# A hybrid decoder step on one core: the routing of the next expert moved from chunks 10 to 12 of a trip to chunks 3 to 7

## The reference

```python
def moe_swiglu(x, g, w_router, w_eg, w_eu, w_ed):
    h = rms_norm(x, g)
    hf = h.reshape(-1, D_MODEL)
    logits = (hf @ w_router).astype(jnp.float32)
    top_v, top_i = lax.top_k(logits, TOP_K)
    gates = jax.nn.softmax(top_v, axis=-1)
    combine = jnp.einsum('tk,tke->te', gates, jax.nn.one_hot(top_i, N_EXPERTS, dtype=jnp.float32)).astype(h.dtype)
    y = jnp.zeros_like(hf)
    for e in range(N_EXPERTS):
        he = jax.nn.silu(hf @ w_eg[e]) * (hf @ w_eu[e])
        y = y + combine[:, e:e + 1] * (he @ w_ed[e])
    return x + y.reshape(x.shape)
```

## Time and profile before

| | |
|---|---|
| median of three runs | 1713.35 us (1709.89 to 1715.0) |
| profiled execution: time, span | 1716.68 us, 1714.6 us |
| TensorE busy | 1556.1 us (91%), 7880 matmuls |
| VectorE busy | 1274.8 us (74%) |
| ScalarE busy | 959.4 us (56%) |
| GpSimd busy | 147.8 us (9%) |
| HBM read | 422.55 MB |
| mean granted TensorE clock | 0.939 of full speed |

### The profile page before, as it was taken

The page is one execution under the profiler, slowest core; times in us unless marked ns, Lnnn a source line. Parts: engine busy times, 40 slices in busy tenths (PEclk is TensorE's granted clock), DMA queues, the critical chain, the costliest instruction groups (busy, mean ns, idle before and its releaser), DMA issues.

```text
span 1714.6 us, 22193 instructions
## 1 busy us (share of the span) xinstructions
PE 1556.1 (91%) x7880; PEld 1305.6 (76%) x7880; DVE 1274.8 (74%) x1277; ACT 959.4 (56%) x999; POOL 147.8 (9%) x135
## 2 busy tenths in 40 slices
PE   6776899999978889979989979979997997997998
PEld 5764899999956868858868868868876885886886
DVE  5998645446784468868868868868886885886886
ACT  5411543344553357656656656657665765765664
POOL 5561111012210100000000000000000000000000
PEclk8888999999987889989989989999998998998999
DMA  8821245444450269969969969987996996996993
GB/s 316 152 94 54 74 148 183 150 144 166 146 206 1 77 258 355 346 248 355 358 263 352 354 249 364 353 320 289 347 349 246 352 354 240 357 353 249 352 350 140
DMA packets 64321, 431.38 MB, mean 252 GB/s; under 512 B 7861, under 2 KB 10165, under 8 KB 13712
## 3 DMA queue, kind: packets, MB, share of 16 engines
q1 hardware_dynamic: 57312, 412.38, 64.0%
q0 software_dynamic: 3616, 12.28, 3.1%
q10 hardware_dynamic: 3344, 6.05, 1.0%
HBM read 422.55 MB, written 9.14 MB: 252 GB/s over the span
## 4 chain that ended last, share of the span: by engine, by line
PE 79%; DVE 11%; DMA 4%; ACT 3%; issue 2%; POOL 1%; ACTq 0%; DVEq 0%; POOLq 0%
PE bank L333 24%; PE bank L335 23%; PE bank L334 23%; DMA xt<-h_rows,slot_row 3%; DVE odd L1173 2%; DVE C L1173 2%; DVE w_lo L1118 2%; PE bank L718 1%; PE bank L355 1%; DVE w_lo L1394 1%; ACT w_hi L1013 1%; PE bank L589 1%; PE bank L669 1%; DVE C L1186 1%; PE bank L700 1%
## 5 line engine op out<-in xcount | busy, mean ns | idle before, releaser
L1394 DVE TENSOR_TENSOR w_lo<-land,w_hi 128x2048 fp32r<-128x2048 f32 x224 | 504.0, 2288 | 106.3 <-ACT w_hi L1013 105.3
L1013 ACT CAST w_hi<-land 128x2048 fp32r<-128x2048 f32 x224 | 417.3, 1910 | 3.5 <-issue 3.5
L333 PE MATMUL bank<-w_hi,xe_hi 128*128 128x512 f32 x896 | 366.3, 409 | 0.6 <-DVE xe_lo L1478 0.6
L334 PE MATMUL bank<-w_lo,xe_hi 128*128 128x512 f32 x896 | 355.5, 397 | 0.0
L335 PE MATMUL bank<-w_hi,xe_lo 128*128 128x512 f32 x896 | 355.5, 397 | 0.0
L1016 ACT CAST d_hi<-land 128x2048 fp32r<-128x2048 f32 x112 | 214.0, 1911 | 117.2 <-PE bank L335 117.2
L1489 DVE TENSOR_TENSOR d_lo<-land,d_hi 128x2048 fp32r<-128x2048 f32 x112 | 256.7, 2292 | 30.5 <-ACT d_hi L1016 25.4
L335 PEld LDWEIGHTS bank<-w_hi,xe_lo 128*128 128x128 f32 x896 | 169.1, 189 | 40.8
L333 PEld LDWEIGHTS bank<-w_hi,xe_hi 128*128 128x128 f32 x896 | 169.6, 189 | 34.2 <-issue 1.0
L334 PEld LDWEIGHTS bank<-w_lo,xe_hi 128*128 128x128 f32 x896 | 169.8, 190 | 33.0
L333 PE MATMUL bank<-d_hi,heT_hi 128*128 128x512 f32 x448 | 184.1, 411 | 4.8 <-DVE heT_lo L1511 4.8
(11 more groups left out here) (243 smaller groups left out, 2221.9 us busy)
## 6 DMA issues: line engine op xcount, KB each, us to landing
land<-in_w_expert SPq DMA_DIRECT2D x336, 1024.0 KB, 5.2
land<-in_w_dense SPq DMA_DIRECT2D x54, 1024.0 KB, 4.8
rel_rows<-rb POOLq DMA_DIRECT2D x1, 3072.0 KB, 38.0
bias<-rel_rows ACTq DMA_DIRECT2D x4, 512.0 KB, 5.4
X<-in_x SPq DMA_DIRECT2D x4, 288.0 KB, 6.0
out_y<-X SPq DMA_DIRECT2D x2, 576.0 KB, 2.8
Us<-in_state POOLq DMA_DIRECT2D x1, 1088.0 KB, 9.4
out_conv_s<-Us POOLq DMA_DIRECT2D x1, 1088.0 KB, 6.5
```

Of the source, the lines that this page charges most:

```text
L333: pe.matmul(out, w[0], x[0], start=start, stop=False)
L334: pe.matmul(out, w[0], x[1], start=False, stop=False)
L1013: act.copy(w_hi[n % RING][:], land[(DENSE + u) % LAND][:]).then_inc(hi_done, 1)
L1394: dve.tensor_tensor(w_lo[n % RING][:], land[slot][:], w_hi[n % RING][:].bitcast(F32), ALU.subtract).then_inc(split, 1)
```

## The change

The constant `GATES_AT` becomes `TURN_AT = 3` and `SCATTER_AT = 10`. Within a trip:

- the transposes of `pick` stand at the end of chunk 3 (before: 10) and go to bank 4 in place of 7; TensorE no longer waits there for the eighth sum;
- `place(trip+1)` stands in chunk 4 (before: 11);
- `slot_rows` stands at the end of chunk 6 (before: 11) and goes to bank 5; it no longer waits for the copy of `PT`;
- `slot_row_of` stands in chunk 7 (before: 12) and GpSimd's fetch follows it; it also copies the gate to a new tile `next_gate`, from which `slot_gate` is written at the end of the trip, in place of a read of bank 7;
- ScalarE's copy to `PT` stands in chunk 10 (before: 11) and waits for the eighth `back` to be done (semaphore `y_done`), since `back` reads the old `PT` up to then;
- TensorE waits for that copy before `gather` writes bank 4 in chunk 13.

```diff
-GATES_AT = KT_D + 2
+TURN_AT = 3
+SCATTER_AT = KT_D + 2
...
+               ("slot_gate", [SLOTS, 1], F32), ("next_gate", [SLOTS, 1], F32), ("slot_of", [P, 3, PASSES * NE + 1], F32),
...
             def turn_picks():
                 for j, (t0, nt) in enumerate(TT):
-                    last = pe.transpose(bank[7][:, t0:t0 + nt], pick[0:nt, j, :], ident[0:nt, 0:nt])
+                    last = pe.transpose(bank[4][:, t0:t0 + nt], pick[0:nt, j, :], ident[0:nt, 0:nt])
...
                         with pe.If(trip < n_trips - 1):
+                            pe.wait_ge(PT_ready, trip + 2)
                             gather(trip + 1, 0)
...
-                    if ch == GATES_AT:
-                        pe.wait_ge(y_added, trip * KT_D + KT_D)
+                    if ch == TURN_AT:
                         turn_picks()
-                    if ch == GATES_AT + 1:
+                    if ch == TURN_AT + 3:
                         with pe.If(trip < n_trips - 1):
                             pe.wait_ge(P_ready, trip + 2)
-                            pe.wait_ge(PT_ready, trip + 2)
-                            slot_rows(bank[7])
+                            slot_rows(bank[5])
...
-                    if ch == GATES_AT + 1:
+                    if ch == SCATTER_AT:
                         act.wait_ge(PT_done, trip + 1)
-                        act.copy(PT[:, :], bank[7][:, 0:T]).then_inc(PT_ready, 1)
+                        act.wait_ge(y_done, trip * KT_D + KT_D)
+                        act.copy(PT[:, :], bank[4][:, 0:T]).then_inc(PT_ready, 1)
...
                 dve.wait_ge(rows_placed, n)
+                dve.tensor_copy(next_gate[:], src[:, 1:2]).then_inc(gate_kept, 1)
                 dve.tensor_scalar(slot_row[:], src[:, 0:1], -1.0, float(T), ALU.mult, ALU.add).then_inc(rows_ready, 1)
...
-                    if ch == GATES_AT + 1:
+                    if ch == TURN_AT + 1:
                         with dve.If(trip < n_trips - 1):
                             dve.wait_ge(PT_done, trip + 1)
                             place(trip + 1)
...
-                    if ch == GATES_AT + 2:
+                    if ch == TURN_AT + 4:
                         with dve.If(trip < n_trips - 1):
-                            slot_row_of(trip + 2, bank[7])
+                            slot_row_of(trip + 2, bank[5])
...
                     dve.wait_ge(oe_ready, trip * 2 + 4)
-                    dve.tensor_copy(slot_gate[:], bank[7][:, 1:2]).then_inc(gates_ready, 1)
+                    dve.wait_ge(gate_kept, trip + 2)
+                    dve.tensor_copy(slot_gate[:], next_gate[:]).then_inc(gates_ready, 1)
```

More of the change, by code:

```diff
@@ L174, in build @@
                ("PT", [SLOTS, T], F32R), ("tok", [P, 3, 2], F32), ("slot_row", [SLOTS, 1], I32),
-               ("slot_gate", [SLOTS, 1], F32), ("slot_of", [P, 3, PASSES * NE + 1], F32),
+               ("slot_gate", [SLOTS, 1], F32), ("next_gate", [SLOTS, 1], F32), ("slot_of", [P, 3, PASSES * NE + 1], F32),
                ("gate_of", [P, 3, PASSES * NE + 1], F32), ("lg", [P, 6, 3, NE], F32), ("rt", [P, 3], F32),
                ("cmp", [P, 2, 3, NE, NE], F32), ("top", [P, 16], F32), ("trips", [1, 2], I32)]
-        (d_hi0, d_hi1, d_lo0, d_lo1, oe_hi, oe_lo, pick, PT, tok, slot_row, slot_gate, slot_of, gate_of, lg, rt,
+        (d_hi0, d_hi1, d_lo0, d_lo1, oe_hi, oe_lo, pick, PT, tok, slot_row, slot_gate, next_gate, slot_of, gate_of, lg, rt,
          cmp_, top, trips, xe_hi, xe_lo, xt, silu_g, he, heT_hi, heT_lo) = phase(
@@ L236, in build @@
                              "sel_ready", "pos_done", "route_ready"))
-        h_stored, rt_inverse, htok_scaled, rows_placed, rows_ready, gates_ready, xt_ready, oe_hi_ready, zero_made, pick_zero, zero_stored, rows_seen = (
+        h_stored, rt_inverse, htok_scaled, rows_placed, rows_ready, gates_ready, xt_ready, oe_hi_ready, zero_made, pick_zero, zero_stored, rows_seen, gate_kept = (
             sem(n) for n in ("h_stored", "rt_inverse", "htok_scaled", "rows_placed", "rows_ready", "gates_ready",
                              "xt_ready", "oe_hi_ready", "zero_made", "pick_zero",
-                             "zero_stored", "rows_seen"))
+                             "zero_stored", "rows_seen", "gate_kept"))
         P_ready, gathered, xe_hi_ready, xe_ready, PT_done, PT_ready = (
@@ L674, in slot_rows @@
                 for j, (t0, nt) in enumerate(TT):
-                    last = pe.matmul(out[:, 0:2], pick[0:nt, j, :], tok[0:nt, j, :], start=(j == 0), stop=(j == 2))
+                    last = pe.matmul(out[:, 0:2], pick[0:nt, j, :], tok[0:nt, j, :],
+                                     start=(j == 0), stop=(j == 2))
                 last.then_inc(rows_placed, 1)
@@ L1464, in _ @@
             slot_row_of(1, bank[0])
-            dve.tensor_copy(slot_gate[:], bank[0][:, 1:2]).then_inc(gates_ready, 1)
+            dve.wait_ge(gate_kept, 1)
+            dve.tensor_copy(slot_gate[:], next_gate[:]).then_inc(gates_ready, 1)
             seq(dve.tensor_reduce(top[:, 8:9], STAT[:, 64:64 + NE], AX.X, ALU.max))
```

## The result

The changed kernel takes 1651.09 us in the median of 4 runs (1650.11 to 1652.78), against 1711.94 us for the kernel before (4 runs, 1709.89 to 1715.0): 0.9644 of its time, interval 0.9626 to 0.9662. It is faster by 61 us. The forecast was 1653 us, with a range of 1641 to 1668. The profiled execution took 1650.97 us.

The account below looks back on a forecast made before the run. TensorE bounds the trip's inside, and slot row, fetch and transpose the borders. Saving 68.8 us there less 8.0 for clock falls gives 60.8 off 1716.68, 1655.9; less 3.3 to the median, 1652.6 us, range 1641 to 1668.

Parts of the forecast that it names:

- The bound: Expert loop: TensorE bounds the trip's inside; slot row, fetch, transpose bound the border between trips, 64.4 us in seven waits.
- The rebuilt border: Border between trips without the wait for fetched rows: 15.7 us each, 109.9 for seven against 178.7, saving 68.8 us.
- The clock: Pause between `down(12)` and `down(13)`: TensorE's clock falls at five borders of seven, costing 8.0 us; bounds 0 and 22.
- that wait of 3.70 us: Near case in the earlier trace, before 75.44 us: clock 0.77 over 70 to 85 us, 6.9 us at low level.
- rival 1: The clock stays up at all borders between trips: 1644.6 us; chance 20%.
- The rule on transposes: Transposes don't count as busy for TensorE's clock as matmuls do; all seven borders would fall, 11.2 us instead of 8.0.
- The fetch: Row numbers written in chunk 7 give the fetch some 50 us, against at most 0.94 + 8.4; all seven waits go.
- The edits costed at nothing: Moved work in chunks 3, 4, 6, 7, 10 and the fetch among weight loads: cost 0 each.
- rival 2: The clock falls at every border and for as long as before: 1667 us; chance 15%.
- 3: Weight loads become the bound at a 325 GB/s ceiling, each trip 135.5 us: 1703 us; chance 5%.
- 4: The fetch holds up a weight load in chunks 7 and 8; at 20 us hold-up, 1748 us; chance 2%.
- 5: The fetch waits behind something on GpSimd's queue till the border: 1713 us; chance 3%.

Follow-up runs that it names:

- the thinner pause: Changed kernel with one transpose of `xt` per half in place of four at the seven borders between trips: 1650.3 us, ratio 0.9629.

## Why the prediction was right

**The bound.** It said that the border is bound by slot row, fetch and transpose, and nothing else in the change carries the gain. The run with all parts but the early fetch shows it: 1.0006.

**The rebuilt border.** It gave 15.7 us; measured 15.8. The steps hold one by one. Counted from the end of `down(12)` the prediction had `down(13)` start after 3.0 us, `he` of chunk 0 after 15.25 and the first turn after 15.65; measured are 3.03 (994.34 - 991.31), 15.31 (1006.62) and 15.78 (1007.09). The idle time before that turn was to be 1.6 us and is 1.30, since TensorE's 48 matmuls took 11.45 us and not 11.0. So 68.0 us in place of 68.8 came from the borders. This worked because no duration in it was new: each piece was read from the border as it stood, and only the wait in it was taken out.

**The clock.** Here a term was off. Forecast were falls at five borders, 6.9 us long, 1.6 us net each, 8.0 in all. Measured: one fall, 3.5 us long, with about 0.1 us net. What a fall costs was mis-sized as well as how many there are: the 3.5 us at the low level hold TensorE back by 1.5 us, which the wait for `he` hides almost whole. The earlier trace rows was a poor likeness: that wait of 3.70 us had no transposes in it and stood in another stage, with narrower matmuls (288 columns) around it; which of these differences matters is not shown. The prediction put the idle time in the pause at about 1 us, and it is 1.09 + 0.64 = 1.7, so the clock stayed up at six borders in spite of more idle time than was reckoned with. With this term at 0.1 the forecast would have been 1644.7 us, which is rival 1.

**What cancelled it.** Two smaller things that the sum took as nothing. The profiled execution lost 2.3 us outside the borders, part of it in a stage that the change does not touch. And the sum took the changed kernel's median 3.3 us below its profiled execution, since that was so before; after, the two are 0.1 us apart. Together with 0.7 us that the borders fell short besides the clock that makes 7.9 - 0.7 - 2.3 - 3.4 = 1.5 us, the distance between 1652.6 and 1651.09. That the total came within 2 us of the measured one is luck, for its terms were not that good: 7.9 us of error one way met 6.4 us the other.

**The rule on transposes.** The prediction weighed what the Trainium skill, "TensorE: Matmul & The Clock Gate", Part 4, says, by which all seven borders would fall. The trace of the changed kernel shows one of seven, and over all the versions with these short pauses none to four. So it does not hold as a forecast for pauses of this length, which are only in part transposes. Where the same pauses were filled with matmuls, no border fell, which is what the rule would lead one to expect. Whether a transpose itself counts was not settled by the thinner pause.

**The fetch.** The lead was put at "some 50 us" and is 41, which is 4.6 chunks of 8.9 us and not six. Its time was bounded by 0.94 + 8.4 us. The landing times are counted from the start of the issue (1010.93 + 6.6 is 1017.53, when TensorE went on), so the rows gave 8.4 in all; measured are up to 11.0 us, with an issue of 2.65 in them. The lead was shorter and the fetch longer than reckoned with, and neither cost anything, as 41 us cover 11. With a lead of one chunk it did cost: 22 us of wait in the seven borders of the run with the fetch one chunk ahead.

**The edits costed at nothing** (`place`, `PT`, the row numbers in chunk 7, the fetch among the loads): confirmed together, by 1.0006 for all of them without the early fetch, and for the fetch by doubling it. None was run by itself.

**The rivals.** Rival 1 had the clock right and would have been nearer on the profiled execution's borders; rival 2 is refuted by the clock of 1.00 at six of seven; 3 and 4 by the absence of any wait for a weight with two fetches; 5 by the fetch at 950.07.

## What to carry to other kernels

The wait between loop turns was worth about what it lasted here (64.4 us of wait, 68.0 us of borders), because the other engines stood still with TensorE and their queues behind it were as long as before. Moving its source up by several chunks took it away whole; one chunk of lead was too little here, since the same fetch took longer inside the trip than at the border. Before forecasting such a move, rebuild the border from its own rows without the wait, ask which engine's queue comes last then, and look for a long operation in that queue that nobody needs yet: `he` behind a 2.29 us subtraction was worth 1.4 us per border. A clock term should be given with what hides it, as a slow stretch beside another engine's lateness can be free.

## What the runs showed of the hardware

**GpSimd's issue waits for VectorE's subtraction.** The same indirect DMA was issued in 0.94 us at the border, and in 2.65 us in chunk 7. VectorE in the changed kernel at that time:

```profile
949.20 0.41 DVE L1504 TENSOR_TENSOR he<-silu_g,bank 128x256 f32<-128x256 f32 x1
949.62 2.29 DVE L1493 TENSOR_TENSOR d_lo<-land,d_hi 128x2048 fp32r<-128x2048 f32 x1
```

The subtraction, which reads two operands from SBUF (the memory on the chip in which the tiles lie), ends at 951.91, the issue at 952.72, 0.81 us behind. With the fetch one chunk ahead of its use the issue began right after the subtraction did:

```profile
988.61 2.29 DVE L1493 TENSOR_TENSOR d_lo<-land,d_hi 128x2048 fp32r<-128x2048 f32 x1 [0.38 <-ACT d_hi L1017]
```
```profile
988.69 3.03 POOL L1650 DMA_INDIRECT xt<-h_rows,slot_row  x1 [128.58 <-DVE slot_row L1464]
```

It ends at 991.72, 0.82 us behind the subtraction's end. The kernel with two fetches has both cases side by side:

```profile
951.37 2.29 DVE L1493 TENSOR_TENSOR d_lo<-land,d_hi 128x2048 fp32r<-128x2048 f32 x1
954.92 4.50 DVE L1396 TENSOR_TENSOR w_lo<-land,w_hi 128x2048 fp32r<-128x2048 f32 x2 [0.93 <-ACT w_hi L1014]
```
```profile
951.81 2.66 POOL L1650 DMA_INDIRECT xt<-h_rows,slot_row  x1 [124.97 <-DVE slot_row L1464]
954.77 0.94 POOL L1652 DMA_INDIRECT xt<-h_rows,slot_row  x1 [0.30 <-issue]
```

The first begins within the subtraction and ends 0.81 us behind it (954.47 against 953.66). The second begins 0.15 us ahead of the next subtraction and takes 0.94 us. This reads as if the issue's own last 0.8 us could only begin when VectorE's subtraction was done. All the traces fit it: in the twelve profiled executions 64 issues began during such a subtraction, 0.07 to 0.47 us after its start, and every one ended 0.81 to 0.85 us behind its end; the other 40 took 0.94 to 1.08 us. The Trainium skill, "GPSIMD Engine Reference", section "1. Specifications", says that GpSimd shares its SBUF interfaces with VectorE, with contention where a VectorE instruction has two SBUF inputs; the traces fit that, and put a price on it, 1.7 to 2.1 us here. No run varied VectorE's instruction alone, so this is what the rows fit and not what was tested. On this kernel it was hidden.

**A fetch is slower among the loads.** From issue to landing 8.1 us in the median and 11.0 at most inside a trip, against 6.6 and 8.4 at a border. Part of it is the longer issue: in the run with two fetches the second of each pair, whose issue took 0.94 us, landed 7.5 us after it in the median (7.2 to 8.4). Of the 1.5 us more in the median about 0.6 thus go with the issue, and 0.9 with the loads or the other fetch beside it.
